# When VectorE makes the low part of the next weight block: at the head of a block, or between its stages

## The chip, the cores and the metric

The kernel runs on one core of one Trainium2 chip. The metric is the device time of one execution in microseconds (us); less is better. Three runs of the kernel before gave 3169.3, 3171.38 and 3172.1 us, so the median is 3171.38 us.

## The reference, cut to what matters

One inference step of a decoder layer, for a prompt of 512 tokens (with 16 learned tokens in front) and 8 sequences of 8 tokens: 592 token columns in all, 2048 wide. The layer has two groups of eight heads of width 128, a gated DeltaNet (GDN) and an HGRN2 (HG), then an output projection and a squared-ReLU MLP.

```python
def token_mixer(h, ...):
    proj = h @ w_in                                   # 2048 x 8208
    qg, kg, vg, zg, bg, ag, qh, fh, ih, zh = split(proj)
    q, k, v = l2norm / silu(causal_conv(qg | kg | vg))
    beta, g = sigmoid(bg), -exp(a_log) * softplus(ag + dt_bias)
    fgate = lb + (1 - lb) * sigmoid(fh)
    gh, kh = log(fgate), 1 - fgate
    o1 = gdn_chunked(q, k, v, beta, g, state)         # triangular solve and state per chunk
    o2 = hgrn2_chunked(qh, kh, ih, gh, state)         # decay by pairs, state per chunk
    og = gated_head_norm(o1, zg);  oh = gated_head_norm(o2, zh)
    return concat(og, oh) @ w_out
x = x + token_mixer(rmsnorm(x));  u = relu(rmsnorm(x) @ w_up);  x = x + (u * u) @ w_down
return rmsnorm(x), states
```

## The kernel before, in words

All large products keep float32 accuracy on a faster format: each operand is split into a rounded high part and a low part that holds the rest, and TensorE adds three products (high by high, high by low, low by high). A weight *unit* is half a column tile of weights, 8 tiles of 128 by 128. SyncE loads it into one of four slots of `w_raw`, ScalarE rounds it into `w_hi` (helper `hi`, L1307), and VectorE subtracts to get `w_lo` (helper `lo`, L1740). `w_hi` and `w_lo` have two slots each. The load of a unit waits for the low part of the unit four before it.

The change touches the part of the program in which the columns of `w_in` are multiplied. For each of the eight heads every engine walks through 16 *blocks* (j = 0 to 15). In block j TensorE multiplies unit 2 + j of the head (48 matrix products of 296 columns, L872, six for each of the 8 weight tiles). It waits at the start of the block for that unit's low part. ScalarE and VectorE prepare unit 3 + j, which TensorE uses in the next block. ScalarE can begin its rounding when the unit before TensorE's present one is done, so at about the start of block j.

The recurrent work of the heads is laid between the weight tiles. `HG_STAGES` and `GDN_STAGES` give each stage a position: 8 times the block, plus the tile after which TensorE does its part. Blocks 0 to 7 carry the HG stages of the head before, and blocks 8 to 15 the GDN stages of the present head. The positions fall like this (block: stage at tile):

- HG: block 0 `gdn_out` 2, `gates` 3, `conv_in` 6; block 1 `turn_v` 0; block 2 `turn_k` 2, `stw` 4, `diag` 6; block 3 `l1` 0, `l2` 3, `l4` 7; block 4 `l8` 3, `l16` 7; block 5 `l32` 2, `l64` 6; block 6 `o` 2, `out` 6; block 7 `st0` 2.
- GDN: block 8 `gates` 0; block 9 `norms` 6, `rows` 7; block 10 `scores` 4, `turn_v` 5, `turn_k` 6, `ws0` 7; block 11 `turn_r0` 0, `t1` 1, `p2` 2, `tp2` 3, `t2` 4, `p4` 5, `tp4` 7; blocks 12 and 13 the further levels; block 13 also `vn0` 7; blocks 14 and 15 `st0` and four rounds of `ws`, `vn`, `st`, the last of which is `ws_4` at tile 4 of block 15.

VectorE follows the order of its program strictly. At an even block it first takes the finished product out of PSUM (`evacuate`, L1823 to L1829), then it makes the low part, then it does its share of the stages of that block, then in blocks 4 to 6 the taps of a convolution (L1842 and L1846). Two stages are long on it. `gates` of HG (L1979 to L1998) is a chain that goes back and forth with ScalarE's exponentials and logarithms and ends at L1998. `gates` of GDN (L1857 to L1869) is another such chain and ends at L1869. The first head has no HG stages; there `small_start`, `small_rest` and `small_end` make the decay rates in blocks 0, 1 and 4. After the eighth head the last HG stages are run by other code, and the output projection and the MLP follow.

Of the kernel before, what the change touches and what calls it, by code (L numbers as in the profile page):

```python
# [48 lines left out]
UK = 8  # L49
RAW = 4  # L50
# [153 lines left out]
def hymba_kernel(nc, io):  # L204
    ctx = ExitStack()
    with ctx:
# [640 lines left out]
        def bank(i, a, n, rows=P):  # L847
            return mx[0:rows, i, a:a + n]
# [884 lines left out]
        def _(dve):  # L1733
# [3 lines left out]
            def lo(u_, ring, base=None):  # L1737

                dve.wait_ge(s_hi, u_ + 1)
                TT(w_lo[:, ring % 2], w_raw[:, ring], w_hi[:, ring % 2].bitcast(F32), ALU.subtract).then_inc(s_lo, 1)  # L1740
# [42 lines left out]
            def small_start():  # L1783
                cdve.done(TT(lb_tmp[:, 0, :], lb_raw, lb_raw, ALU.subtract), "lb0")
                cact.wait(dve, "lb", 0)
                cdve.done(dve.reciprocal(lb_tmp[:, 0, :], lb_tmp[:, 1, :]), "lb1")
                cdve.wait(dve, "lb1", 0)
                cdve.done(TT(lb_tmp[:, 1, :], lb_tmp[:, 1, :], lb_tmp[:, 0, :], ALU.mult), "lb2")
                cdve.wait(dve, "lb2", 0)
                cdve.done(TT(lb[:, :], lb_tmp[:, 1, :], lb_tmp[:, 1, :], ALU.subtract), "lb3")  # L1790
                cdve.wait(dve, "lb3", 0)
                cdve.done(TS(one_lb[:, :], lb[:, :], -1.0, 1.0, ALU.mult, ALU.add), "one_lb")
                dve.wait_ge(s_unit, 2)
                cdve.wait(dve, "rstd", 0)
                TT(halves(bag), mains(0)[0:16], halves(rstd[0:16, :]), ALU.mult).then_inc(s_evac, 1)
                dve.wait_ge(s_rates, 32)
                dve.wait_ge(s_evac, 1)
                cdve.done(TS(bag, bag, dt_bias[:, 0:1], None, ALU.add), "dt")

            def small_rest():  # L1800
                cact.wait(dve, "b_exp", 0)
                cdve.done(TS(bag1, bag1, BIG, None, ALU.min), "clamp")
                cdve.done(STT(bag2, bag, -1.0, bag, ALU.mult, ALU.max), "abs")
                cact.wait(dve, "s_ln", 0)
                cdve.done(STT(bag, bag, 0.0, bag2, ALU.max, ALU.add), "soft")
                cdve.wait(dve, "soft", 0)
                cdve.done(TS(bag, bag, a_exp[:, 0:1], -1.0, ALU.mult, ALU.mult), "g")
                cdve.wait(dve, "g", 0)
                cdve.done(scan(b_rows[:, :], bag, 16), "b")
                cdve.wait(dve, "b", 0)  # L1810
                cdve.done(end_arg(bag2, b_rows, 16), "e_arg")

            def small_end():
                cpe.wait(dve, "cols", 0)
                dve.tensor_copy(b_col[:, :, :], bank(0, 0, 16 * NW).rearrange("p (c n) -> p c n", c=NW))
                cdve.done(dve.tensor_copy(e_col[:, :, :], bank(1, 0, 16 * NW).rearrange("p (c n) -> p c n", c=NW)), "cols")

            def evacuate(tile, j, h):

                p = mains(tile)  # L1820
                if j >= 3:
                    dst = {3: gz, 4: hq, 5: hf, 6: hv, 7: hz}[j]
                    TT(halves(dst[:, :]), p, halves(rstd[:, :]), ALU.mult).then_inc(s_evac, 1)  # L1823
                    return
                n1 = HALF - NS
                TT(u[:, j, 0:UP0].rearrange("p (b t) -> p b t", b=SB)[:, :, PRE:USEQ], seq(p[:, 0, :]), seq(rstd),
                   ALU.mult)
                TT(u[:, j, UP0 + PRE:UP0 + PRE + n1], p[:, 0, NS:HALF], rstd[:, NS:HALF], ALU.mult)
                TT(u[:, j, UP0 + PRE + n1:UW], p[:, 1, :], rstd[:, HALF:N], ALU.mult).then_inc(s_evac, 1)  # L1829

            def convolve(j, h):
                o = conv[:, j, :]
                for t in range(TAPS):
                    if isinstance(h, int):
                        w = conv_w[:, t, j, h:h + 1]
                    else:
                        w = conv_w[:, t, j, bass.ds(h, 1)]
                    x = u[:, j, t:t + CW]
                    if t == 0:
                        dve.wait_ge(s_evac, h * 8 + (2 + j))  # L1840
                        gdve.wait(dve, "conv_in", h)
                        ins = TS(o, x, w, None, ALU.mult)  # L1842
                        ins.then_inc(s_tap, 1)
                    else:
                        dve.wait_ge(s_tap, h * 9 + (3 * j + t))
                        ins = STT(o, x, w, o, ALU.mult, ALU.add)  # L1846
                        if t < TAPS - 1:
                            ins.then_inc(s_tap, 1)
                gdve.done(ins, f"conv_{j}")
# [203 lines left out]
            def history(h):  # L2053
                gpe.wait(dve, "conv_in", h)
                for j in range(3):
                    ins = dve.tensor_copy(u[:, j, 0:UP0].rearrange("p (b t) -> p b t", b=SB)[:, :, 0:PRE],
                                          bank(2, j * P, SB * PRE).rearrange("p (b t) -> p b t", b=SB))
                gdve.done(ins, "conv_in")

            def save_last(h):  # L2060
                dve.wait_ge(s_evac, h * 8 + 4)
                n_ = SB * PRE
                for j in range(3):
                    dve.tensor_copy(last[:, j, 0:n_].rearrange("p (b t) -> p b t", b=SB),
                                    u[:, j, 0:UP0].rearrange("p (b t) -> p b t", b=SB)[:, :, ST:USEQ])
                gdve.done(dve.tensor_copy(last[:, :, n_:n_ + PRE], u[:, :, UW - PRE:UW]), "last")

            def head(h, first):
                for j in range(16):
                    if j % 2 == 0 and not (first and j == 0):  # L2070
                        dve.wait_ge(s_unit, h * 16 + (2 + j))

                        evacuate(j // 2, (j // 2 - 1) % 8, h)
                    if first and j == 0:
                        dve.wait_ge(s_mask, MASK_STEPS)
                    lo(h * 16 + (3 + j), (3 + j) % RAW)
                    if j < 8:
                        for st, pos in HG_STAGES.items():
                            if pos // UK == j:
                                if not first:  # L2080
                                    hg(st, h - 1, h)
                                elif st == "conv_in":
                                    dve.wait_ge(s_padded, 1)
                                    history(0)
                        if first:
                            if j == 0:
                                small_start()
                            if j == 1:
                                small_rest()
                            if j == 4:  # L2090
                                small_end()
                        if j in (4, 5, 6):
                            convolve(j - 4, h)
                        if j == 6:
                            save_last(h)
                    else:
                        for st, pos in GDN_STAGES.items():
                            if pos // UK == j - 8:
                                gdn(st, h, first)

            head(0, True)
            for h in range(1, HEADS):
                head(h, False)
# [16 lines left out]
            for st in HG_STAGES:  # L2120
# [3 lines left out]
                if st in ("l8", "l16"):  # L2124
                    u_ = OUT_U0 + (2 if st == "l8" else 3)
# [275 lines left out]
```

## Time and profile before

| what | value |
| --- | --- |
| median of three runs | 3171.38 us |
| the profiled execution, its own time | 3170.59 us |
| its span on the core | 3168.8 us |
| TensorE matrix products busy | 3014.4 us, 95% |
| VectorE busy | 2033.3 us, 64% |
| ScalarE busy | 1204.5 us, 38% |

The 1.8 us between the profiled execution's own time and its span lie around the span. The eight heads take the stretch from about 67 to 1431 us; the pattern repeats for heads 1 to 7 at about 174 us each. The rest, to the end, is the last HG stages, the output projection and the MLP, in other code.

In a row of a timeline the first number is the start in us, the second the duration in us, then the engine, the line, the operation and its operands; square brackets hold the idle time of the engine just before it, and what ended that.

### The profile page before, as it was taken

The page shows a single profiled execution, that of the slowest core. Times are in us where ns is not written, and L with a number is a line of the kernel's source. Part 1 is how long each engine was busy: PE and PEld are TensorE (multiplying, and loading weights), DVE is VectorE, ACT ScalarE, POOL GpSimd, SP SyncE. Part 2 cuts the span into 40 slices and gives each one's busy share as a digit, 9 for nine tenths or more (in the row PEclk, how much of TensorE's full clock was granted, in tenths as well). Part 3 has the DMA queues.
Part 4 walks back from the last instruction along what each step waited for, and adds up shares of the span by engine and source line. Part 5 has one row for each costly group of instructions (what it writes and reads, how often), then busy time and mean ns, then how long its engine had stood idle before and what let it go on. Part 6 is the DMA issues. An engine that isn't in the chain of part 4 may idle for free.

```text
span 3168.8 us, 52451 instructions
## 1 busy us (share of the span) xinstructions
PE 3014.4 (95%) x22024; PEld 2953.2 (93%) x22024; DVE 2033.3 (64%) x2820; ACT 1204.5 (38%) x1522; POOL 313.6 (10%) x433
## 2 busy tenths in 40 slices
PE   6999989898999999897999999999998999999998
PEld 5998989898989989896999999999998999999998
DVE  4546364545546463646447777777778878888885
ACT  4333323232323232233324444444444444444454
POOL 4010101010110101010111000000000000000021
PEclk8999999999999999998999999999999999999999
DMA  5333454433232333323533454444447666666665
GB/s 185 70 74 62 56 66 58 74 63 75 62 73 64 73 60 58 75 53 99 161 110 112 134 159 139 153 149 146 157 139 251 202 196 196 192 193 195 194 194 186
DMA packets 513498, 392.60 MB, mean 124 GB/s; under 512 B 16400, under 2 KB 483040, under 8 KB 513264
## 3 DMA queue, kind: packets, MB, share of 16 engines
q1 hardware_dynamic: 461664, 268.86, 34.6%
q0 software_dynamic: 22832, 88.39, 7.7%
q10 hardware_dynamic: 28768, 32.00, 3.5%
q8 instruction: 174, 2.85, 0.4%
q14 instruction: 60, 0.49, 0.1%
HBM read 304.87 MB, written 84.33 MB: 123 GB/s over the span
## 4 chain that ended last, share of the span: by engine, by line
PE 82%; DVE 10%; ACT 4%; issue 2%; DMA 1%; POOL 0%; DVEq 0%; ACTq 0%; POOLq 0%
PE main L1219 38%; PE main L872 26%; PE mx L1219 6%; PE mx L1117 2%; PE mx L1016 1%; PE mx L1024 1%; PE mx L948 1%; DVE tmp L1846 1%; PE mx L932 1%; DVE w_lo L1740 1%; ACT w_hi L1307 1%; PE mx L1058 1%; PE mx L983 0%; PE mx L975 0%; ACT tmp L1472 0%
## 5 line engine op out<-in xcount | busy, mean ns | idle before, releaser
L872 PE MATMUL main<-h_hi,w_hi 128*128 128x296 f32 (+1 forms) x2592 | 625.4, 323 | 26.1 <-DVE w_lo L1740 22.8
L1219 PE MATMUL main<-forms_a,w_hi 128*128 128x288 f32 x3072 | 618.7, 297 | 8.6 <-DVE forms_a L2294 4.7
L1219 PE MATMUL main<-forms_b,w_hi 128*128 128x288 f32 x3072 | 613.9, 295 | 7.0 <-DVE forms_b L2294 4.9
L872 PE MATMUL main<-h_hi,w_lo 128*128 128x296 f32 (+1 forms) x2592 | 578.2, 305 | 0.0
L872 PE MATMUL main<-h_lo,w_hi 128*128 128x296 f32 (+1 forms) x2592 | 577.7, 305 | 0.0
L1219 PEld LDWEIGHTS main<-forms_a,w_hi 128*128 128x128 f32 x3072 | 497.7, 190 | 9.5 <-issue 9.3
L1219 PEld LDWEIGHTS main<-forms_b,w_hi 128*128 128x128 f32 x3072 | 492.1, 188 | 8.3 <-issue 5.5
L872 PEld LDWEIGHTS main<-h_hi,w_hi 128*128 128x128 f32 x2592 | 429.1, 197 | 39.3 <-DVE w_lo L1740 25.4
L1219 PE MATMUL main<-forms_a,w_lo 128*128 128x288 f32 x1536 | 456.7, 297 | 0.0
L1219 PE MATMUL main<-forms_b,w_lo 128*128 128x288 f32 x1536 | 452.2, 294 | 0.0
L872 PEld LDWEIGHTS main<-h_hi,w_lo 128*128 128x128 f32 x2592 | 435.3, 195 | 0.0
L872 PEld LDWEIGHTS main<-h_lo,w_hi 128*128 128x128 f32 x2592 | 434.9, 195 | 0.0
L1587 ACT ACTIVATE w_hi<-w_raw 128x1024 fp32r<-128x1024 f32 x256 | 271.3, 1060 | 332.8 <-PE main L1219 225.2
L2241 DVE TENSOR_TENSOR w_lo<-w_raw,w_hi 128x1024 fp32r<-128x1024 f32 x256 | 312.2, 1219 | 65.3 <-PE main L1219 65.3
L1307 ACT ACTIVATE w_hi<-w_raw 128x1024 fp32r<-128x1024 f32 x162 | 170.5, 1052 | 401.0 <-PE main L872 400.9
L1587 ACT ACTIVATE w_hi<-w_sum 128x1024 fp32r<-128x1024 f32 x190 | 201.5, 1061 | 297.1 <-PE main L1219 297.0
L1219 PEld LDWEIGHTS main<-forms_a,w_lo 128*128 128x128 f32 x1536 | 290.6, 189 | 0.0
L1219 PEld LDWEIGHTS main<-forms_b,w_lo 128*128 128x128 f32 x1536 | 289.1, 188 | 0.0
L1740 DVE TENSOR_TENSOR w_lo<-w_raw,w_hi 128x1024 fp32r<-128x1024 f32 x162 | 197.6, 1220 | 114.7 <-ACT w_hi L1307 114.4
L2241 DVE TENSOR_TENSOR w_lo<-w_sum,w_hi 128x1024 fp32r<-128x1024 f32 x190 | 234.0, 1231 | 16.6 <-PE main L1219 16.6
L1219 PE MATMUL mx<-forms_b,w_hi 128*128 128x288 f32 x1024 | 207.0, 296 | 1.7 <-DVE forms_b L2294 1.7
L1219 PEld LDWEIGHTS mx<-forms_b,w_hi 128*128 128x128 f32 x1024 | 164.3, 188 | 2.1 <-issue 2.1
(382 smaller groups left out, 3612.3 us busy)
## 6 DMA issues: line engine op xcount, KB each, us to landing
w_raw<-in_w_in SPq DMA_DIRECT2D x130, 512.0 KB, 8.2
w_raw<-in_w_up SPq DMA_DIRECT2D x128, 512.0 KB, 4.1
w_raw<-in_w_down SPq DMA_DIRECT2D x100, 512.0 KB, 4.5
u_forms<-ub POOLq DMA_DIRECT2D x32, 1152.0 KB, 6.7
z<-x_scratch SPq DMA_DIRECT2D x32, 576.0 KB, 7.5
x_scratch<-z POOLq DMA_DIRECT2D x31, 576.0 KB, 3.1
stage<-u_forms ACTq DMA_DIRECT2D x30, 576.0 KB, 4.0
w_raw<-in_w_out SPq DMA_DIRECT2D x32, 512.0 KB, 4.0
```

The source lines that it names most:

```text
L872: ins = mm(out[:, half, :], w[:, ring, k, :], x[:, kx, half * width:half * width + width], start=first and n == 0, stop=last_ and n == 2)
L932: ins = mm(mx[:, i + half, 0:HALF], ones[:, :], src[:, half * HALF:half * HALF + HALF], start=True, stop=True)
L948: ins = pe.transpose(mxf[:, 512 * i + n_ * P:512 * i + n_ * P + P], src(c), ident[:, :])
L1016: ins = mm(bank(0, 64 * c, 64), xl[:, c, :], left, start=True, stop=True)
L1024: ins = mm(bank(1, 64 * c, 64), tT[:, c, :], pc[:, c, :], start=True, stop=True)
L1058: ins = mm(bank(i, 0, n_ * P), kdt[:, 0, :], vx[:, 4 * i:4 * i + n_, :], start=True, stop=True)
L1117: ins = mm(bank(i % 2, 64 * c, 64), win(hkk, c), hqq[:, ctok(c):ctok(c) + 64], start=True, stop=True)
L1219: ins = mm(out, w[:, k, :], x[:, kx, :], start=i in (0, 1, 3) and k == 0 and n == 0, stop=k == KP - 1 and n == 2, skip_group_check=True)
L1307: A(w_hi[:, ring % 2], w_raw[:, ring], ACT.Copy).then_inc(s_hi, 1)
L1587: A(hi_slot(u_), src, ACT.Copy).then_inc(s_hi, 1)
L1740: TT(w_lo[:, ring % 2], w_raw[:, ring], w_hi[:, ring % 2].bitcast(F32), ALU.subtract).then_inc(s_lo, 1)
L2241: TT(w_lo[:, u_ % 2], src, hi_slot(u_).bitcast(F32), ALU.subtract).then_inc(s_lo, 1)
```

## The change

The low part is no longer made at the head of the block. It is put in a list, and a new function makes it ahead of the first stage of the block whose tile is 4 or more, or after the last stage of the block if there is none.

```diff
+            def low_part(split):
+
+                for u_ in split:
+                    lo(u_, u_ % RAW)
+                split.clear()
+
             def head(h, first):
                 for j in range(16):
                     if j % 2 == 0 and not (first and j == 0):
...
                         evacuate(j // 2, (j // 2 - 1) % 8, h)
                     if first and j == 0:
                         dve.wait_ge(s_mask, MASK_STEPS)
-                    lo(h * 16 + (3 + j), (3 + j) % RAW)
+                    split = [h * 16 + (3 + j)]
                     if j < 8:
                         for st, pos in HG_STAGES.items():
                             if pos // UK == j:
+                                if pos % UK >= UK // 2:
+                                    low_part(split)
                                 if not first:
                                     hg(st, h - 1, h)
...
                                 small_rest()
                             if j == 4:
                                 small_end()
+                        low_part(split)
                         if j in (4, 5, 6):
                             convolve(j - 4, h)
...
                         for st, pos in GDN_STAGES.items():
                             if pos // UK == j - 8:
+                                if pos % UK >= UK // 2:
+                                    low_part(split)
                                 gdn(st, h, first)
+                        low_part(split)
```

## Rows read from the trace of the kernel before

**Rows 1.** The page, part 1: busy time, share, instructions.
```profile
PE 3014.4 (95%) x22024; PEld 2953.2 (93%) x22024; DVE 2033.3 (64%) x2820; ACT 1204.5 (38%) x1522; POOL 313.6 (10%) x433
```
**Rows 2.** Waits of TensorE over the span: who for whom, total us, times, longest.
```profile
PE mx L1117 <- DVE tmp L2036: 45.2, 24, 4.0
PE main L872 <- DVE w_lo L1740: 22.8, 10, 5.6
```
**Rows 3.** Timeline of TensorE, head 4, end of block 0 to block 2.
```profile
741.64 0.44 PE L872 MATMUL main<-h_hi,w_hi 128*128 128x296 f32 x2
...
742.47 0.71 PE L948 MATMUL mx<-ident,hv 128*128 128x128 f32 x5
...
750.93 0.54 PE L872 MATMUL main<-h_hi,w_hi 128*128 128x296 f32 x2 [2.02 <-DVE w_lo L1740]
```
**Rows 4.** Timeline of VectorE, the same head, blocks 0 and 1.
```profile
735.94 1.22 DVE L1740 TENSOR_TENSOR w_lo<-w_raw,w_hi 128x1024 fp32r<-128x1024 f32 x1 [0.96 <-ACT w_hi L1307]
738.93 0.83 DVE L1947 SCALAR_TENSOR_TENSOR tmp<-tmp,vecs_t 128x592 f32<-128x592 f32 x1 [1.77 <-ACT tmp L1439]
...
748.70 0.78 DVE L1998 TENSOR_TENSOR tmp<-tmp 128x592 f32<-128x592 f32 x1
749.39 0.35 DVE L2056 COPY u<-mx 128x24 f32<-128x24 f32 x3
749.66 1.21 DVE L1740 TENSOR_TENSOR w_lo<-w_raw,w_hi 128x1024 fp32r<-128x1024 f32 x1
```
**Rows 5.** The page, part 6: DMA issues, KB, us from issue to landing.
```profile
w_raw<-in_w_in SPq DMA_DIRECT2D x130, 512.0 KB, 8.2
```
**Rows 6.** Timeline of TensorE, blocks 8 and 9.
```profile
818.52 0.49 PE L961 MATMUL mx<-ident,last 128*27 128x128 f32 x3 [0.49 <-DVE hstate L2045]
...
824.58 0.43 PE L872 MATMUL main<-h_hi,w_hi 128*128 128x296 f32 x2
```
**Rows 7.** Timeline of VectorE, end of block 7 and block 8.
```profile
817.15 1.22 DVE L2045 TENSOR_TENSOR hstate<-hstate,mx 128x1024 f32<-128x1024 f32 x1
...
821.20 1.23 DVE L1860 TENSOR_SCALAR tmp<-tmp 128x1848 f32<-128x1848 f32 x1
...
829.12 0.77 DVE L1869 TENSOR_TENSOR gz<-gz,tmp 128x592 f32<-128x592 f32 x1
```
**Rows 8.** Timeline of ScalarE, block 8.
```profile
819.43 1.74 ACT L1373 ACTIVATE tmp<-tmp 128x1848 f32<-128x1848 f32 x1
```
**Rows 9.** Timeline of VectorE, block 2 to block 3 of HG.
```profile
761.35 0.86 DVE L2020 COPY_PREDICATED tmp<-imask,mx 128x640 f32<-128x640 uint8 x1
763.24 1.23 DVE L1740 TENSOR_TENSOR w_lo<-w_raw,w_hi 128x1024 fp32r<-128x1024 f32 x1 [1.03 <-ACT w_hi L1307]
```
**Rows 10.** Timeline of TensorE, levels `l1`, `l8` and `l32`.
```profile
766.89 2.39 PE L1117 MATMUL mx<-tmp 128*128 128x64 f32 x10 [4.02 <-DVE tmp L2036]
...
782.14 1.33 PE L1117 MATMUL mx<-tmp 128*128 128x64 f32 x10 [0.24 <-DVE tmp L2036]
...
791.42 1.10 PE L1117 MATMUL mx<-tmp 128*128 128x64 f32 x8 [1.25 <-DVE tmp L2036]
```
**Rows 11.** Stretches: us, busy of PE, PEld, DVE, ACT, POOL, granted clock, DMA.
```profile
751.50:755.00 3.50, 3.50 (x16) 3.48 (x15) 2.59 (x5) 0.00 (x0) 0.00 (x0) 0.51 0.36 96
...
766.90:772.10 5.20, 5.20 (x22) 5.20 (x23) 3.25 (x8) 0.97 (x2) 0.00 (x0) 0.50 0.36 79
```
**Rows 12.** Timeline of TensorE after the heads: another wait for a low part.
```profile
1508.75 0.85 PE L872 MATMUL main<-h_hi,w_hi 128*128 128x288 f32 x2 [5.58 <-DVE w_lo L1740]
...
1512.76 0.44 PE L872 MATMUL main<-h_hi,w_lo 128*128 128x288 f32 x2
```
**Rows 13.** Timeline of ScalarE, first head, start of block 1.
```profile
75.26 1.06 ACT L1307 ACTIVATE w_hi<-w_raw 128x1024 fp32r<-128x1024 f32 x1 [10.69 <-PE main L872]
```
**Rows 14.** Timeline of VectorE, first head, block 1, and TensorE, block 3.
```profile
85.73 0.90 DVE L1780 TENSOR_TENSOR tmp<-b_rows 16x64 f32<-16x64 f32 x3
...
89.63 0.54 PE L872 MATMUL main<-h_hi,w_hi 128*128 128x296 f32 x2 [1.34 <-DVE w_lo L1740]
```

## The prediction

> **What bounds the kernel now.** I read the page's busy shares first: matrix products fill 95% of the span and VectorE 64% [rows 1], so the end is set by TensorE, and a change on VectorE counts only by what it adds to or takes from TensorE's waits. The second view is the list of those waits: 45.2 us for the level products of HG (L1117) on L2036, 22.8 us at the start of a block on the low part [rows 2]. The third is the timeline of TensorE and VectorE side by side through one head. Heads 1 to 7 repeat every 174 us, so one of them, counted seven times, and the first head by itself make the sum. The tail after the eighth head isn't touched.
>
> The thing to see in the timelines is when a low part is needed and when VectorE would now get to it. It is needed at the start of the next block. A pure block is 8 tiles of 0.83 us (741.64 to 742.47 [rows 3]), 6.6 us, and more with stages in it. A stage that takes VectorE longer than that, placed ahead of the low part, makes TensorE wait.
>
> **Block 0 of HG, the dearest place.** Its stages are at tiles 2, 3 and 6, so the low part goes behind `gdn_out` and `gates` and ahead of `conv_in`. Now it is made at 735.94, in time that VectorE spends idle anyway (0.96 us before it, 1.77 us after it), so the chain of the gates, which starts when ScalarE is done at 738.93, gets no earlier by its going. That chain ends with L1998 at 748.70, and the next instruction starts at 749.39 [rows 4]. There the low part will now start; with its 1.21 us and the 0.06 us that TensorE took after it (749.66 + 1.21 = 750.87, against 750.93 [rows 3, 4]) TensorE goes on at 750.66. It is ready for block 1 at 741.64 [rows 3]: a new wait of **9.0 us**. Behind the low part queue the copies of `conv_in` (L2056), 1.2 us later; their readers are in block 2 and later and have time.
>
> **Block 1.** Its only stage, `turn_v` at tile 0, comes ahead of the low part. TensorE starts the block at 750.66 and has 7.3 us of work in it (741.64 to 748.91, where the wait before 750.93 begins [rows 3]). The transposes, ScalarE's copy and VectorE's product of this stage would have to take 5 us together after tile 0 to make the low part late, and the widest pass in these rows (1848 columns) takes 1.23 us [rows 7]. So the old wait of **2.0 us** is gone, and what is late next is nothing.
>
> **Block 3.** The first level waits 4.02 us [rows 10]. VectorE ends `diag` at 762.2, then waits 1.03 us for ScalarE's rounding, then makes the low part until 764.5, and only then the arguments of the level [rows 9]. With the low part behind `l2` these arguments are ready 2.2 us sooner; ScalarE's exponential must wait for its own rounding, which ends at 763.2, and then starts at 763.2 instead of 765.3: **2.0 us** saved, 2.0 us of wait left. The low part then goes in ahead of `l4`, a stage with slack.
>
> **Blocks 4 and 5.** `l8` and `l32` wait 0.24 and 1.25 us [rows 10]. `l8` comes ahead of the low part now and loses its wait. The low part of block 5 (1.2 us) leaves the front of `l32` and most of its wait goes, 1.2 us: together **1.4 us** saved.
>
> **Block 7.** Its stage `st0` (two passes of 1.22 us) moves ahead of the low part, which block 8 needs at once. The state is ready at 817.2 instead of 818.4 [rows 7], so the wait of 0.49 us [rows 6] goes. But the low part then ends at 818.4, where block 8 could have begun at 817.2 (818.52 less the wait and one tile): the products of `gates` follow a tile later, at 819.2 instead of 818.52, net **0.7 us** lost.
>
> **Block 8, the GDN gates.** The only stage is at tile 0, so the low part goes behind all of it. The chain is again set by ScalarE: the first clamp starts at 821.20, when the exponential from 819.43 ends [rows 7, 8], so taking the low part from in front of it brings nothing forward. The chain's last instruction starts at 829.12 and ends at 829.9 [rows 7]; the low part ends at 831.0 and TensorE goes on at 831.1. It is ready for block 9 at 824.58 [rows 6] (the 0.7 us above moves both alike): a new wait of **6.5 us**, in all eight heads.
>
> **The rest.** In blocks 2, 6, 9 and 10 the first stage with work on VectorE ahead of which the low part goes is the first or nearly so. In blocks 11 to 14 the stages in front (`tp2`, `tp8`, `tp32`, `st_1`) wait on TensorE's own products of the same block, so the low part still comes some us before the next block; in block 15 it delays `ws_4` by some tenths and frees `ws_3` by as little. Zero, between minus 0.2 and plus 0.3 us a head. Each load of weights waits for the low part of the unit four before; it starts up to 13.5 us later in the two bad blocks, but takes 8.2 us [rows 5] and is due four blocks (over 26 us) later. The slower queues, SyncE's and POOL's, hold nothing else that waits on the moved instruction.
>
> **The clock after a wait.** Two waits of this trace are followed by stretches at a granted clock of 0.51 and 0.50 of full, the 1.2 GHz level [rows 11]. Half of such a stretch is lost: 1.7 us of 3.5 after the 2.02 us wait, 2.6 us of 5.2 after the 4.02 us wait. After a wait of 5.58 us for a low part, 8 pairs of products take 4.0 us (1508.75 to 1512.76 [rows 12]) where 0.28 us a pair (a third of a tile) makes 2.2: 1.8 us. I take 2.0 us for each new long wait (bounds 0 and 2.6; nearest is the 5.58 us row, a wait of the same kind), credit 1.7 us for the wait that goes in block 2, and 2.6 - 1.7 = 0.9 us for the level whose wait halves (bounds 0 and 2.6).
>
> The Trainium skill ("TensorE: Matmul & The Clock Gate", section on the HAM clock gate) says that for modelling the ramp is under 1% of a typical kernel and isn't worth fitting. By that rule the clock terms would be left out and the sum be some 14 us smaller; the rows above speak against leaving it out here, because the ramp would be paid at 16 new waits.
>
> **The sum.** A head of 1 to 7: 9.0 + 2.0 (block 0) - 2.0 - 1.7 (block 1) - 2.0 - 0.9 (block 3) - 1.4 (blocks 4, 5) + 0.7 (block 7) + 6.5 + 2.0 (block 8) = 12.2 us; seven are 85.4. The first head: block 8 gives 6.5 + 2.0. In its block 1 `small_rest` goes ahead of the low part; block 0 ended at 75.2 [rows 13], so block 2 is due at 81.8, and `small_rest` ends at 86.6 (85.73 + 0.90) [rows 14], which ScalarE's answers set; low part to 87.8, wait 6.0 us and 2.0 for the clock, less the 1.3 us of wait at block 3: 6.7. Together 15.2. In all **+100.6 us** on 3170.6 us, the profiled execution's own time (span 3168.8 and 1.8 around it): 3271.2; on the median of the runs, 0.8 us higher, 3272.
>
> **Rivals.** (a) *The clock costs nothing at the new waits.* For it: after the wait of 1.25 us the products aren't slow (8 in 1.10 us against 10 in 1.33 [rows 10]). Each head loses 4.0 less: 8.2 x 7 + 11.2 = 69, so 3240 us. Chance 0.12. (b) *The credits don't come, or the clock costs more.* Level `l1` keeps its wait (2.9 us a head), each long wait costs 2.5: 16.1 x 7 + 16.2 = 129, so 3300 us. Against it: the order in block 3 is plain in the rows. Chance 0.14. (c) *The lead that the long waits give ScalarE and VectorE is kept, and later waits shrink further.* The wait of `l1` goes wholly: 2.0 + 1.7 us a head more, 26 in all, 3246 us. Against it: the levels wait on products of the block before. Chance 0.13. (d) *Faster.* The place is the two `gates` blocks: if the gates chains ended before TensorE's block does, the waits of 9.0 and 6.5 us would not exist and what is left is the credits, 2.0 + 1.7 + 2.9 + 1.4 - 0.7 = 7.3 us a head, 51 us, 3120 us. It decides where a chain ends 7.8 us sooner in block 0 and 5.3 in block 8, and I see nothing that shortens them, since ScalarE paces both. Chance 0.02. (e) *The change doesn't do what it says*, the low part stays in front of the gates and all cancels: 3171 us. The tiles 3 and 0 of the two gates are under 4, so 0.01. The forecast has 0.58.
>
> **Numbers.** 3272 us. All cases but the last two are slower, so the range is made of (a) to (c): 3236 to 3306. Within 0.2% (6.3 us) is about what a measurement of this kernel can't tell from no change. Slower 0.96, same 0.02, faster 0.02.
>
> **What would show it.** Right: in the list of waits L872 on L1740 grows from 22.8 us to some 136 (16 long ones of 6 to 9 us), with the ends of VectorE's L1998 and L1869 just before them; L1117 on L2036 falls from 45.2 to near 21; the level's first wait is 2 us; head to head takes 186 us. Wrong: if blocks 1 and 9 begin with no wait, or if VectorE's gates chain starts earlier than before relative to the block.

## The result and the profile after

The changed kernel takes 3270.1 us (median of four runs, 3253.8 to 3273.4) against 3171.0 us for the kernel before: a ratio of 1.030, 95% interval 1.027 to 1.034 (ratios and intervals below are to the kernel before as well). It is slower by 99 us; 3272 were forecast. The profiled execution took 3269.4 us, with a span of 3267.6.

The page's first part, the same columns as [rows 1]:

```profile
PE 3028.4 (93%) x22024; PEld 2968.8 (91%) x22024; DVE 2033.0 (62%) x2820; ACT 1205.2 (37%) x1522; POOL 307.7 (9%) x433
```

Nothing is added in instructions or in VectorE's work (2033.3 before, 2033.0 now). TensorE is 14.0 us longer busy with the same matrix products (3014.4 to 3028.4), so some of them ran at a lower clock, and the other 85 of the 99 us of span are idle time. Where they lie stands in the list of TensorE's waits (us in total, times, longest), which answers to [rows 2]:

```profile
PE main L872 <- DVE w_lo L1740: 136.5, 25, 9.5
PE mx L1117 <- DVE tmp L2036: 19.8, 10, 2.9
```

The wait for a low part grew by 113.7 us, the level products' wait fell by 25.4, and that of L961, the products of the `gates` stage in block 8, is gone. In the kernel before it stood in the list with

```profile
PE mx L961 <- DVE hstate L2045: 3.4, 7, 0.5
```

Together this is 85 us. So the whole change is in two numbers, 85 us of waits and 14 of clock. (A *slow stretch* below is a stretch in which the granted clock is 0.50, so that half of TensorE's busy time in it is lost.)

The timeline of TensorE in head 4, from the end of block 0 to block 9 (it answers to [rows 3, 6, 10]):

```profile
790.99 0.52 PE L872 MATMUL main<-h_hi,w_hi 128*128 128x296 f32 x2
...
801.41 0.86 PE L872 MATMUL main<-h_hi,w_hi 128*128 128x296 f32 x2 [9.35 <-DVE w_lo L1740]
...
822.82 2.29 PE L1117 MATMUL mx<-tmp 128*128 128x64 f32 x10 [1.86 <-DVE tmp L2036]
...
873.45 0.54 PE L872 MATMUL main<-h_hi,w_hi 128*128 128x296 f32 x2 [1.21 <-DVE w_lo L1740]
...
886.82 0.86 PE L872 MATMUL main<-h_hi,w_hi 128*128 128x296 f32 x2 [6.23 <-DVE w_lo L1740]
```

The wait of 2.0 us at block 2 isn't there, that of `l1` is 1.86 instead of 4.02 us, and `l8` and `l32` don't wait; in their place stand 9.35 us at block 1, 1.21 at block 8 and 6.23 at block 9. VectorE in the same stretch (answers to [rows 4, 7]):

```profile
793.37 0.78 DVE L1984 TENSOR_TENSOR tmp<-tmp 128x592 f32<-128x592 f32 x1 [1.79 <-ACT tmp L1455]
794.06 1.02 DVE L1985 TENSOR_SCALAR tmp<-hf,one_lb 128x592 f32<-128x592 f32 x1
...
799.44 0.77 DVE L1998 TENSOR_TENSOR tmp<-tmp 128x592 f32<-128x592 f32 x1
800.13 1.22 DVE L1740 TENSOR_TENSOR w_lo<-w_raw,w_hi 128x1024 fp32r<-128x1024 f32 x1
801.27 0.36 DVE L2056 COPY u<-mx 128x24 f32<-128x24 f32 x3
...
884.86 0.77 DVE L1869 TENSOR_TENSOR gz<-gz,tmp 128x592 f32<-128x592 f32 x1
885.54 1.22 DVE L1740 TENSOR_TENSOR w_lo<-w_raw,w_hi 128x1024 fp32r<-128x1024 f32 x1
887.14 1.23 DVE L1740 TENSOR_TENSOR w_lo<-w_raw,w_hi 128x1024 fp32r<-128x1024 f32 x1 [0.38 <-ACT w_hi L1307]
```

The low part starts right behind the last instruction of each gates chain, L1998 and L1869, and TensorE goes on 0.06 us after it ends. In block 8 the next one follows 1.6 us later: two units are made almost back to back, the first far too late.

### The profile page after: what moved, and what is told of

It is laid out like the page before. It is cut to its first block, busy times and chain, and to the rows that moved or that the text cites. A ratio compares the mean times of both kernels' runs of the same rounds, so it can differ in the third digit from the quotient of the medians.

```text
span 3267.6 us, 52451 instructions
## 1 busy us (share of the span) xinstructions
PE 3028.4 (93%) x22024; PEld 2968.8 (91%) x22024; DVE 2033.0 (62%) x2820; ACT 1205.2 (37%) x1522; POOL 307.7 (9%) x433
## 4 chain that ended last, share of the span: by engine, by line
PE 84%; DVE 9%; ACT 5%; issue 1%; DMA 0%; POOL 0%; DVEq 0%; ACTq 0%; POOLq 0%
PE main L1219 36%; PE main L872 28%; PE mx L1219 6%; PE mx L1117 2%; PE mx L948 1%; PE mx L1016 1%; PE mx L1024 1%; PE mx L932 1%; DVE w_lo L1740 1%; DVE tmp L1846 1%; PE mx L983 1%; PE mx L975 1%; PE mx L1058 0%; ACT tmp L1375 0%; ACT tmp L1377 0%
## 5 line engine op out<-in xcount | busy, mean ns | idle before, releaser
L872 PE MATMUL main<-h_hi,w_hi 128*128 128x296 f32 (+1 forms) x2592 | 635.2, 327 | 139.8 <-DVE w_lo L1740 136.5
L872 PEld LDWEIGHTS main<-h_lo,w_hi 128*128 128x128 f32 x2592 | 441.6, 198 | 0.0
L2253 DVE TENSOR_TENSOR w_lo<-w_sum,w_hi 128x1024 fp32r<-128x1024 f32 x190 | 234.0, 1232 | 16.6 <-PE main L1219 16.6
```

Source lines behind the costliest of these rows:

```text
L872: ins = mm(out[:, half, :], w[:, ring, k, :], x[:, kx, half * width:half * width + width], start=first and n == 0, stop=last_ and n == 2)
L2253: TT(w_lo[:, u_ % 2], src, hi_slot(u_).bitcast(F32), ALU.subtract).then_inc(s_lo, 1)
```

## The experiments

"The low part of block j" and "the unit of block j" are those that VectorE makes in block j; TensorE uses them in block j + 1. A block is "put right" when its low part is made at the head of the block again. Five kernels start from the changed one (block 0 put right, block 8, both and two more, busy waits, the memset), four from the fastest found so far. Times are medians of four runs, if nothing else is said. Heads are counted from 0, so head 3 is the fourth. The diffs are cut to what matters (`...` marks what is left out), and what follows a `#` in them is a note of this text.

**Block 0 alone put right.**

```diff
                     split = [h * 16 + (3 + j)]
+                    if j == 0:
+                        low_part(split)
```

> The changed kernel with the low part at the front again in block 0 of HG alone, ahead of the gates. My theory: the long wait at block 1 (9.35 us in the trace after) goes with the slow clock behind it (about 1.7 us), in seven heads. Since turn_v still stands in front of the low part of block 1, that low part comes after ScalarE's rounding at the end of the gates and after a pass of 1.36 us, so block 2 waits 3 to 4 us with its own slow stretch. Net 5.5 us a head, so 38 us less than after: 3225 to 3240 us. Rival (the wait is only moved, the gates chain paces the head): all of the 9.35 us comes back at block 2, time stays within 10 us of 3270.

It took 3241.0 us (ratio 1.022, 1.021 to 1.024), 29 us less than the changed kernel and just over the range expected. In six heads the wait moved as thought: none at block 1, 3.88 us at block 2. Head 3 waits 11.27 us there instead; without these 7.4 us more the run would lie in its range. TensorE is 5.1 us longer busy than in the changed kernel (3028.4 to 3033.5), so the clock gave nothing back. The reason for head 3 is on VectorE (timeline of that head):

```profile
609.40 0.36 DVE L2056 COPY u<-mx 128x24 f32<-128x24 f32 x3
617.63 1.36 DVE L2003 TENSOR_TENSOR tmp<-tmp,seq_rows 128x1152 f32<-128x1152 f32 x1 [7.87 <-DMA mix_scratch<-tmp]
618.90 1.22 DVE L1740 TENSOR_TENSOR w_lo<-w_raw,w_hi 128x1024 fp32r<-128x1024 f32 x1
```

`turn_v` waits for the store of the GDN output, which took 16.6 us here and 7.9 in head 4 of the same run. The low part of block 1 is behind that stage, so TensorE waits for a DMA. The rival (all comes back) falls.

**Block 8 alone put right.** The same edit with `if j == 8`.

> The changed kernel with the low part at the front again in block 8 alone, ahead of the GDN gates. My theory: the wait of 6.23 us at block 9 goes in all eight heads, with about 2 us of slow clock each: 66 us less, 3204 us (3195 to 3215). Rival (the clock costs nothing after such a wait): only 8 x 6.23 = 50 us less, 3220 us.

3185.9 us (1.005, 1.004 to 1.007): 84 us less, more than either side thought. The trace splits it. The low part's wait fell from 136.5 to 86.6 us, which is 8 times 6.23:

```profile
PE main L872 <- DVE w_lo L1740: 86.6, 17, 9.5
```

And TensorE was busy for 2993.2 instead of 3028.4 us, so 35 us came from the clock, 4.4 a head. Only about 2.0 of these are the slow stretch right after the wait, as in head 4 of the changed kernel (stretch, its length, then busy time and instructions of PE, PEld, DVE, ACT and POOL, the granted clock, DMA share, GB/s):

```profile
886.80:890.80 4.00, 3.98 (x16) 3.98 (x17) 1.23 (x1) 0.31 (x1) 0.00 (x0) 0.50 0.44 84
```

Most of the rest lies behind the stage `rows`. The changed kernel has a second slow stretch there in all eight heads, in head 4 some 15 us after the restart:

```profile
901.50:904.80 3.30, 3.30 (x15) 3.30 (x14) 3.30 (x10) 1.82 (x3) 0.00 (x0) 0.50 0.00 0
```

In head 4 of the kernel before the clock is low there too:

```profile
836.00:840.00 4.00, 4.00 (x19) 3.67 (x18) 3.90 (x11) 2.04 (x4) 0.00 (x0) 0.62 0.20 58
```

With block 8 put right it is full:

```profile
846.00:850.00 4.00, 4.00 (x24) 3.28 (x23) 3.14 (x6) 2.09 (x3) 0.00 (x0) 1.00 0.39 104
```

The same stage, with the same 0.6 us wait in it, is followed by a slow stretch in seven heads of the kernel before, in eight of the changed one and in one of this run (head 0). Summed from the slow stretches of the traces, 16 us of clock went right behind the waits, 12 us behind `rows` and 7 us at `l1` (three slow stretches of the changed kernel against two shorter ones here), which is the 35. Why the stretches at `rows` and `l1` went as well isn't shown.

**The four bad places put right.** The same edit with `if j in (0, 1, 7, 8)`: the low part stays in the middle of the block only where it did no harm.

> The changed kernel with the low part at the front in blocks 0, 1, 7 and 8 (so also ahead of small_rest in the first head), in the middle in the others. My theory: what is left are the credits of blocks 3 to 5: 2.1 us of wait at l1, 0.24 at l8 and 1.25 at l32, and about 1 us of clock, 4.5 us in seven heads, 31 us less than the kernel before: 3140 us (3130 to 3150). The 2.0 us wait at block 2 is back. Rival (blocks 11 to 15 lose what 3 to 5 win): 3171 us.

3140.5 us (0.990, 0.989 to 0.992), 30 us faster than the kernel before. The waits of TensorE for the low part and for the levels:

```profile
PE main L872 <- DVE w_lo L1740: 22.8, 10, 5.6
PE mx L1117 <- DVE tmp L2036: 19.7, 10, 2.7
```

The first is back to its old 22.8, the second keeps the 25.5 us that the change won, and TensorE's busy time is 4.8 us less than before (3014.4 to 3009.6). These two are the 30 us. That is the credit side of the forecast by itself, and it leaves no room for a cost of more than some 2 us in the moves of the other blocks, 9 to 15 above all, which weren't tried one by one.

**TensorE kept busy in the waits.**

```diff
+                for _ in range(warm):
+                    mm(mx[:, 3, 0:HALF], h_hi[:, 0, 0:P], h_hi[:, 0, 0:HALF], start=True, stop=True)
...
+                    warm = 62 if j == 0 and not first else 40 if j == 8 else 0
+                    if j == 8 and not first:
+                        hact.wait(pe, "oln", h - 1)      # TensorE waits for ScalarE's step "oln"
```

> The changed kernel, and TensorE does idle work in the two long waits: behind block 0 (heads 1 to 7) 62 products of 296 columns into a free PSUM bank, 8.5 us, and behind block 8 (all heads) 40 of them, 5.5 us; nothing reads them. The waits stay as long as they are, but TensorE is busy in most of them. My theory (about 2 us are lost after each long wait to the 1.2 GHz level of the clock): the slow stretches after 15 of the 16 waits go, 15 x 1.7 to 2.0 = 25 to 30 us less than after, 3240 to 3245 us. Rival (the clock costs nothing, or depends on the phase alone): 3270 us, or a little more for the extra products.

3231.6 us (1.020, 1.018 to 1.022), 38.5 us less than the changed kernel, though it does more work (754 products more) and its low parts are as late to within half a microsecond. In head 4 of it, TensorE idles 0.92 us where the changed kernel idles 9.35, and the 5 us around the restart are at full clock:

```profile
785.56 0.54 PE L872 MATMUL main<-h_hi,w_hi 128*128 128x296 f32 x2 [0.92 <-DVE w_lo L1745]
```

```profile
785.00:790.00 5.00, 4.44 (x33) 4.44 (x34) 2.81 (x6) 0.70 (x1) 0.00 (x0) 1.00 0.55 69
```

So the clock is a real part of the loss. Summing busy time times one less the granted clock over slices of 1 us from 60 to 1660 us gives 69.4 us lost to the clock in the changed kernel, 30.1 in this one and 51.8 in the kernel before: the whole gain of this run is clock, 39 us. It is again more than the stretches right behind the 15 filled waits, which lost some 32 us. By this measure the changed kernel lost 17.6 us more to the clock than the kernel before, where busy time grew by 14.0; the two agree to some us only.

**The unit of block 1 made inside the gates.** On top of the kernel with blocks 0, 1, 7 and 8 put right: ScalarE and VectorE make this unit, the one that block 2 needs, inside the `gates` stage of block 0, and no longer in block 1.

```diff
                     done(A(ho[:, :], ho[:, :], ACT.Exp, scale=-1.0), "zsig")      # ScalarE
+                    if nxt is not None:
+                        hi_at(nxt, 16, 3 + 1)
...
-                    hi_at(h, 16, 3 + j)
+                    if first or j != 1:
+                        hi_at(h, 16, 3 + j)
...
                     done(TT(hz[:, :], hz[:, :], ho[:, :], ALU.mult), "zs")         # VectorE
+                    if nxt is not None:
+                        lo(nxt * 16 + (3 + 1), (3 + 1) % RAW)
...
-                    split = [h * 16 + (3 + j)]
+                    split = [h * 16 + (3 + j)] if first or j != 1 else []
```

> As the kernel with the low part in front in blocks 0, 1, 7 and 8, and besides the unit of block 1 is rounded by ScalarE inside the gates of block 0 (after the last exponential of zsig, where it waits 2.1 us for the scan), and its low part made by VectorE after zs. My theory: block 2 waits no more, 2.0 us and 1.7 us of clock in seven heads, 26 us less than without it: 3115 us (3105 to 3125). Rival (1.2 us more in the gates chain come back as a wait of the transposes of turn_k, and the clock stays as it is): 3135 to 3145 us.

3120.3 us (0.984, 0.983 to 0.986), 20 us less than without it. The low part's waits fell from 22.8 to 8.6 us, so the wait at block 2 is gone in all seven heads. Busy time fell from 3009.6 to 2994.2 us, which is 15 us of clock. Head 3 gives some of it back: it waits 7.1 us at the products of `stw` (L1103), where the kernel without this edit waits 3.6. There `turn_v` waits again for the store of the GDN output, as it does in the first experiment (16.6 us in this run):

```profile
PE mx L1103 <- DVE tmp L2012: 10.9, 8, 7.1
...
PE main L872 <- DVE w_lo L1743: 8.6, 3, 5.6
```

**The first level's arguments made early.** On top of that: VectorE makes `arg1` ahead of the `diag` copy, and ScalarE takes the exponential of `l1` ahead of its rounding in block 3. `level_args` holds the two subtractions that make the arguments.

```diff
                 elif stage == "diag":
+                    level_args(1)
                     W(hpe, "diag")
...
-                    if first or j != 1:
+                    if first or j not in (1, 3):
                         hi_at(h, 16, 3 + j)
...
                                 hg(st, h - 1, h)
+                                if st == "l1":
+                                    hi_at(h, 16, 3 + j)
```

> As the kernel before it in this list, and besides the arguments of the first level are made ahead of the diag copy, and ScalarE takes the exponential of level 1 ahead of the rounding of block 3. My theory: the wait of 1.9 us at l1 falls to about 0.3 us and its slow stretch goes, 3 us in seven heads: 21 us less, about 3095 us (3085 to 3105). Rival (the clock's phase alone decides the slow stretches): only 11 us less.

3089.4 us (0.975, 0.973 to 0.976): 31 us less than the run before it, where 21 were expected. The levels' waits fell by 14.3 us, to 6.0 (three waits, none in the seven repeated heads), and busy time fell from 2994.2 to 2975.9 us, which is 18 us of clock:

```profile
PE mx L1117 <- DVE tmp L2049: 6.0, 3, 2.7
```

This is the fastest version, 81 us faster than the kernel before and 181 faster than the changed one. The rival (the clock's slow stretches don't go with the wait) falls.

**Two small terms by themselves.** Each on top of the fastest version: the low part behind `small_rest` in the first head, and behind `st0` in block 7.

```diff
-                    if j in (0, 1, 7, 8):
+                    if j in (0, 7, 8) or j == 1 and not first:      # the one
+                    if j in (0, 1, 8) or j == 7 and first:          # the other
```

> The fastest kernel so far (3089.4 us), with the low part behind small_rest again in block 1 of the first head, as in the changed kernel. My theory (the term of 6.7 us of the prediction): a wait of 5.8 us at block 2 with 1 to 2 us of slow clock, less the 1.34 us that block 3 waited: 6 to 7 us more, 3095.5 to 3096.5. Rival (the start has slack for it): 3089 to 3091.

3098.8 us (3094.9 to 3100.9), 9.4 us more. The wait at block 2 of the first head is 5.81 us, as thought. The profiled execution took 7.0 us more than that of the fastest version (3094.9 against 3088.0): the waits for a low part grew by 4.4 us (8.7 to 13.1) and TensorE's busy time by 2.5 (2975.9 to 2978.4), which is clock. The four runs reach from just under the forecast to 5 us above it.

> The fastest kernel so far (3089.4 us), with the state update of block 7 ahead of the low part, as in the changed kernel. My theory (the term of 0.7 us a head): a wait of 1.2 us at block 8 in the place of 0.49, 5 us more in seven heads, 3094 us. Rival (the wait of 1.2 us brings slow clock too, 1.7 us a head): 3106 us.

3100.4 us (3098.2 to 3104.7), 11 us more; between theory (5) and rival (17). The low part's waits grew from 8.7 to 17.1 us and the 3.4 us of L961 went, 5.0 us net, as thought; 4.8 us more are TensorE's busy time, so clock. The added slow stretches don't stand right behind the new wait but some 19 us later, behind `rows`: in five of the seven heads, against two in the fastest version. The wait itself, in head 3:

```profile
621.77 0.54 PE L872 MATMUL main<-h_hi,w_hi 128*128 128x296 f32 x2 [1.21 <-DVE w_lo L1745]
```

**The memset held back.** One line on the changed kernel; GpSimd waits for the end of the gates chain before it clears `ha`.

```diff
+                hdve.wait(pool, "kd", h)
                 hpool.done(pool.memset(ha, 0.0), "zero")
```

> The changed kernel, with GpSimd's memset of ha held back until VectorE has finished the gates chain (kd). My theory: L1985 took 0.52 us before and 1.02 us after because in the changed kernel this memset (0.62 us) falls on it; with the memset held back L1985 takes 0.52 us again in all heads, the long wait at block 1 falls from 9.35 to 8.9 us, and the time by some 3 us, less than one run can tell. Rival (L1985 is slow for another reason): it stays at 1.02 us.

One run, 3268.1 us, which can't tell 3 us. The trace can: the instruction (now in line 1986) is back to 0.52 us in all eight heads, and the long wait is 8.85 us in all seven. The changed kernel has the same test in it: in head 3 its memset starts at 607.98, after L1985 (606.66) has ended, and there L1985 takes 0.52 us and the long wait is 8.86. First the changed kernel, then this one (ns, least, median, most):

```profile
L1985 DVE TENSOR_SCALAR tmp<-hf,one_lb x8: 522/1018/1130, 238.0 to 1539.0; 128x592 f32<-128x592 f32 x8
```

```profile
L1986 DVE TENSOR_SCALAR tmp<-hf,one_lb x8: 519/520/522, 239.8 to 1540.6; 128x592 f32<-128x592 f32 x8
```

## Why the prediction was right, step by step

The mechanism is the forecast one: each new wait for a low part stands where the prediction said, ends 0.06 us after the low part, and is within some 0.5 us of its size. Without the clock the sum has 86.8 us of waits, and the trace 85.

- *Block 0, 9.0 us.* Right in place; by the same reckoning (block 1 is due at 791.9, restart at 801.4) it is 9.5 us. The 0.5 us are L1985, which the step took as unchanged. The rest of the chain kept its lengths.
- *Block 1, a credit of 2.0.* The wait is gone in all seven heads. But this holds only because block 1 itself starts late: with block 0 put right, the same order of stages in block 1 gave a wait of 3.88 us.
- *Block 3, a credit of 2.0.* 4.02 to 1.86 us: 2.2.
- *Blocks 4 and 5, 1.4.* Both waits are gone, 0.24 and 1.25 us: 1.5.
- *Block 7, 0.7 lost.* 1.21 in the place of 0.49 us: 0.7. Shown alone it also cost 4.8 us of clock in seven heads, which the step left out.
- *Block 8, 6.5 us.* The profile's idle time is 6.23 us; from the due time (6.06 us after the products of L961, which start at 874.37, so 880.43) to the restart at 886.82 it is 6.4. Right.
- *The rest, zero.* TensorE's list of waits has no new entry. But the sentence that the queues hold nothing else that waits on the moved instruction left out a link: the later load of weights makes the GDN store shorter, and that brings GpSimd's memset onto L1985 (last section). These are the 0.5 us of block 0, in six of the seven heads.
- *The first head, 6.0 us at block 2.* 5.80 us.
- *The clock.* The sum had 13.8 us net, and busy time grew by 14.0. That agreement is of the sum, not of its terms. The stretch after each long wait was sized well: 4.4 us at 0.50 of the clock after the wait of 9.35 us, 4.0 after the one of 6.23, so 2.2 and 2.0 us (the row of the second stands with the second experiment, that of the first just below). The credit at `l1` was taken as 0.9 us in every head. It came to that on average (the slow stretches there lost 16.4 us in the seven heads before and 10.2 after), but by luck: before, every head had one, of 1.7 to 2.7 us lost; after, the wait of 1.86 us is followed by none in heads 1, 2, 6 and 7 and by one of about 6.8 us, 3.4 lost, in heads 3 to 5. Both stretches of head 4 of the changed kernel, behind the wait of 9.35 us and behind that of `l1`:

```profile
801.40:805.80 4.40, 4.39 (x18) 4.37 (x19) 0.93 (x4) 0.70 (x1) 0.00 (x0) 0.50 0.41 77
...
822.80:829.40 6.60, 6.58 (x28) 6.58 (x29) 4.33 (x9) 1.39 (x2) 0.00 (x0) 0.51 0.06 15
```

  The heads of one run differ by it: from one wait at block 8 to the next it is 184.3 to 184.7 us in the one case and 187.2 to 187.8 in the other, and never the 186 that the prediction named. The clock is also the likely reason why one run of the changed kernel took 3253.8 us and the others 3269.4 and more: its mean granted clock is 0.964 against 0.960 and 0.961, which over 3270 us is some 10 of the 16 us (an estimate from these clocks). No trace of that run was taken, so where it lies isn't shown.
- *The rivals.* That the clock costs nothing (3240 us) is refuted by the run with busy waits. That credits don't come (3300) is refuted by the kernel with four blocks put right. That later waits shrink further and that of `l1` goes wholly (3246) is refuted by its 1.86 us. Whether the change could be faster was to be decided by whether the gates chains end before the block does. They don't; with the low part ahead of them the same idea is 30 us faster.

## What to carry to other kernels

An instruction that another engine needs at a fixed time has a due time, and its place among the stages should be chosen by that and by how long the stages ahead of it take, with their waits counted. A position in the other engine's count of tiles says nothing of this: `gates` stood at tile 3 of 8 and took VectorE past the end of the block. To judge a move, read for each block when the moved result is due and when the last stage now ahead of it ends; blocks that gain and blocks that lose can then be separated, and here that turned 99 us lost into 30 us won.

## What the runs showed of the hardware

**What a wait costs in clock isn't all right behind it.** Keeping TensorE busy in 15 waits took away 39 us of clock loss, some 2.6 us a wait, and removing eight waits took away 35, 4.4 a wait, where the stretch right after each loses 2.0 to 2.2 us. The same stage with the same short wait is followed by a slow stretch in one kernel and none in another. What decides it in a given place wasn't found.

**A moved subtraction made a memset collide.** When a low part is made, a slot of `w_raw` comes free and its next load starts. In the kernel before, that load (issued at 737.19, 10.4 us to its landing) ran beside the store of the GDN output, issued at 740.95. GpSimd's memset is behind that store, and came at 748.66, after the one-input instruction L1985 (743.81). The DMAs of 735 to 750 us in the kernel before (queue, form, KB, us from issue to landing):

```profile
w_raw<-in_w_in SPq DMA_DIRECT2D x1, 512.0 KB, 10.4
...
mix_scratch<-tmp POOLq DMA_DIRECT2D x1, 296.0 KB, 7.5
```

In the changed kernel the slot is freed late: one load of weights has landed at 789.6, the next is issued at 801.38, and the store, issued at 791.20 between the two, is done in a third of the time:

```profile
mix_scratch<-tmp POOLq DMA_DIRECT2D x1, 296.0 KB, 2.5
```

So the memset comes early, 0.07 us after the start of L1985, which ran from 794.06 to 795.08, 1.02 us instead of 0.52:

```profile
794.13 0.62 POOL L759 MEMSET tmp<- 128x640 f32 x1
```

The held-back memset shows that the collision is what lengthens L1985. The Trainium skill ("SBUF — State Buffer", section "SBUF: two separate sides") says that the port pair that VectorE and GpSimd share is an exclusive lock: a VectorE operation in a mode that uses both ports and a GpSimd operation don't overlap, and the one that starts first has the pair for its whole length. By that L1985 could be longer by up to the memset's 0.62 us if the memset had the pair. It was longer by 0.50, and the memset kept its 0.62, so the size agrees. The order doesn't follow from the records, in which L1985 starts first, and no run shows in which mode it works. In head 5 they differ: the memset's record starts only at the end of a L1985 of 1.13 us, and the one-element instruction of GpSimd before it takes 1.05 us instead of 0.18; there too L1985 takes 0.52 with the memset held back.

**The store lands after the load of weights that is in flight.** The store of the GDN output (296 KB, issued by GpSimd) took 12.8 us in head 3 and 7.5 in head 4 of the kernel before, 3.8 and 2.5 in the changed one, 16.6 and 7.9 with block 0 put right. The eleven traces hold 77 of these stores. In the 24 with no load of weights (512 KB, issued by SyncE) in flight at their issue it took 2.4 to 3.0 us. In the 47 with one in flight it took 3.2 to 12.8 us, in the 6 with two 16.6 to 17.1, and in all 53 it landed after the load that was in flight had landed, mostly 0.8 us after it (0.3 to 2.3). No run changes the loads alone, so why it is so isn't shown. In most heads this time costs nothing. It counts where something urgent stands behind the stage that waits for the store, as the low part of block 1 did, and in head 3 it costs TensorE 3.6 to 7.6 us at L1103 in the faster kernels.
